# A decoder block on one core: fifteen weight pairs in place of twelve, shorter head turns, and x kept in DRAM

## The reference

```
proj = x @ w_in                               # 1024 -> 6656 channels: q | k | v | cb | cc | ch | g_conv | g_attn
y_conv = cb * conv3(cc * ch)                  # causal depthwise filter of width 3
scores = q @ k.T / 8 + alibi, window 128      # 16 query heads, 4 key/value heads of 64; 8 blocks of 128 tokens
p = exp(scores - m);  probs = p / (sum(p) + exp(sink - m))     # m = max(scores, sink)
y_attn = probs @ v
mix = (sigmoid(g_conv) * y_conv + sigmoid(g_attn) * y_attn) @ w_out
x = layer_norm(ALPHA * x + mix)
x = layer_norm(ALPHA * x + (silu(x @ w_gate) * (x @ w_up)) @ w_down)
```

## Time and profile before

| | |
|---|---|
| median of 3 runs | 1355.69 us |
| the profiled execution | 1358.13 us, span 1356.3 us |
| PE busy | 1340.0 us, 99% |
| DVE, ACT, POOL busy | 848.1, 528.0, 724.8 us |
| granted TensorE clock, mean | 0.996 |
| head turns | about 300 to 630 us of the span |
| first layer norm | about 650 to 710 us |

### The profile page before, as it was taken

One profiled execution on the slowest core, in us unless ns is written; L12 is line 12 of the kernel. 1 busy time (PEld: TensorE's weight loads), 2 busy tenths in 40 slices (PEclk: granted clock), 3 DMA queues, 4 the chain that ended last, 5 costly groups with the idle time before them and its releaser, 6 DMA issues. The chain is left out here.

```text
span 1356.3 us, 18062 instructions
## 1 busy us (share of the span) xinstructions
PE 1340.0 (99%) x6506; PEld 1176.5 (87%) x6506; DVE 848.1 (63%) x1167; ACT 528.0 (39%) x973; POOL 724.8 (53%) x487
## 2 busy tenths in 40 slices
PE   9999999999999999999899999999999999999997
PEld 8888888888888888888788888888888888888886
DVE  5665555576867778787968754545546455464547
ACT  6422322336565565755345332232322313223143
POOL 5588788721222121336682775563756637566374
PEclk9999999999999999999999999999999999999999
DMA  6111222121111111112330221211212112111113
GB/s 187 48 55 55 62 63 63 51 59 48 32 34 45 47 32 32 47 48 78 109 93 1 70 71 47 71 54 39 70 46 70 53 40 70 46 59 58 47 55 125
DMA packets 128816, 80.58 MB, mean 59 GB/s; under 512 B 8816, under 2 KB 123504, under 8 KB 128752
## 3 DMA queue, kind: packets, MB, share of 16 engines
q1 hardware_dynamic: 128752, 79.73, 19.8%
HBM read 75.53 MB, written 4.19 MB: 59 GB/s over the span
## 5 line engine op out<-in xcount | busy, mean ns | idle before, releaser
L828 POOL TENSOR_TENSOR w_lo<-raw,w_hi 128x512 fp32r<-128x512 f32 x80 | 110.3, 1379 | 204.0 <-ACT w_hi L1201 204.0
L679 POOL TENSOR_TENSOR w_lo<-raw,w_hi 128x1024 fp32r<-128x1024 f32 x28 | 68.5, 2447 | 219.9 <-ACT w_hi L887 209.9
L1664 DVE TENSOR_TENSOR res<-res,ps 128x512 f32<-128x512 f32 x128 | 87.2, 687 | 59.8 <-PE ps L1835 59.8
L1833 PE MATMUL ps<-hid_hi,wd_hi 128*128 128x512 f32 x320 | 121.5, 380 | 0.1
L1834 PE MATMUL ps<-hid_lo,wd_hi 128*128 128x512 f32 x320 | 121.3, 379 | 0.0
L1835 PE MATMUL ps<-hid_hi,wd_lo 128*128 128x512 f32 x320 | 121.3, 379 | 0.0
L2127 PE MATMUL ps<-act_hi,w_hi 128*128 128x512 f32 x320 | 121.3, 379 | 0.0
L2128 PE MATMUL ps<-act_lo,w_hi 128*128 128x512 f32 x320 | 121.3, 379 | 0.0
L2129 PE MATMUL ps<-act_hi,w_lo 128*128 128x512 f32 x320 | 121.3, 379 | 0.0
L1833 PE MATMUL ps<-act_hi,w_hi 128*128 128x512 f32 x272 | 104.5, 384 | 0.0
L1834 PE MATMUL ps<-act_lo,w_hi 128*128 128x512 f32 x272 | 103.1, 379 | 0.0
(11 more groups left out here) (262 smaller groups left out, 3590.1 us busy)
## 6 DMA issues: line engine op xcount, KB each, us to landing
raw<-in_w_in SPq DMA_DIRECT2D x28, 512.0 KB, 3.8
raw<-in_w_in SPq DMA_DIRECT2D x48, 256.0 KB, 3.0
raw<-in_w_gate SPq DMA_DIRECT2D x40, 256.0 KB, 2.8
raw<-in_w_up SPq DMA_DIRECT2D x40, 256.0 KB, 3.2
raw_d<-in_w_down SPq DMA_DIRECT2D x20, 512.0 KB, 3.4
raw<-in_w_out SPq DMA_DIRECT2D x16, 512.0 KB, 4.0
xs<-in_x SPq DMA_DIRECT2D x8, 512.0 KB, 6.9
out<-rows SPq DMA_DIRECT2D x7, 512.0 KB, 2.7
```

The costliest lines, as they stand in the source:

```text
L828: pool.tensor_tensor(wide(ring(w_lo, n)), src, fp(wide(ring(w_hi, n))), ALU.subtract).then_inc(pl_s, 1)
L1664: dve.tensor_tensor(tile, tile, bank, ALU.add).then_inc(add_s, 1)
L1833: pe.matmul(bank, w_h(t), hi, start=(t == 0), stop=False)
```

## The change

- `PLAIN = (3,)`: 15 pairs in place of 12; the odd (gc, cb) tiles of turns 0 to 2 leave the head turns, which shrink to 8 units and 8 steps for a block. Turn 3 keeps 12 units.
- New due times for short turns. On VectorE `probs_low` of a block stands at 16.3 and `gate_attention` at 24.35 steps after its start, `normalise` at 7.5.
- `sc` and `exps` become two buffers `sc_even` and `sc`, used in turn; the exponentials overwrite the scores, one element to the left. The sink column is written to both.
- x goes to DRAM (`x_away`) by two DMAs of 2 MB in the prologue and comes back by 16 DMAs of 256 KB in the output stage; `x_sum` is gone.
- Weight slots of the head turns swap parity (`head_slot`, `before_in_slot`), since an odd number of pairs ends in the other slot.
- In the first pair, GpSimd's third sum is made one place earlier. Around the first layer norm, `mean`, `variance` and `spread` are at other steps, and the normalisation is spread over more output units.

```
-PLAIN = (0, 1, 2, 3)
+PLAIN = (3,)
...
+SAME_SLOTS = HEAD_TILES.index((PLAIN[0], "gc", 1))
+
+
+def head_slot(t):
+    return (t + 1) % 2 if t < SAME_SLOTS else t % 2
...
-PE_STEPS = sorted([(block_at(b, 0), "scores", b) for b in BLOCKS] + [(block_at(b, 14, 11), "turn", b) for b in BLOCKS]
-                  + [(block_at(b, 20, 15), "values", b) for b in BLOCKS])
+PE_STEPS = sorted([(block_at(b, 0), "scores", b) for b in BLOCKS] + [(block_at(b, 14, 12.5), "turn", b) for b in BLOCKS]
+                  + [(block_at(b, 20, 20.4), "values", b) for b in BLOCKS])
...
-    [(block_at(b, 16.2, 13), "turn", b) for b in BLOCKS],
-    [(block_at(b, 22.2, 17.2), "values", b) for b in BLOCKS],
+    [(block_at(b, 16.2, 16.3), "turn", b) for b in BLOCKS],
+    [(block_at(b, 22.2, 24.35), "values", b) for b in BLOCKS],
...
-            exps = sb(st, "exps", [P, G * 2 * P + 1])
+            sc_even = sb(st, "sc_even", [P, G, 2 * P + 2])
...
-            sc = sb(st, "sc", [P, G, 2 * P + 1])
+            sc = sb(st, "sc", [P, G, 2 * P + 2])
...
+        x_away = nc.dram_tensor("x_channels", (P, DT, S), F32).ap()
...
+            sp.wait_ge(x_kept, 8)
+            sp.dma_start(x_away[:, :, half(1)], res[:, :, half(1)]).then_inc(x_stored, 16)
...
+            sp.wait_ge(x_sum0, 8)
+            sp.dma_start(x_away[:, :, half(0)], res[:, :, half(0)]).then_inc(x_stored, 16)
...
+            def x_again(h, m):
+
+                sp.wait_ge(m_lo_s, DT * h + m + 1)
+                sp.dma_start(res[:, m, half(h)], x_away[:, m, half(h)]).then_inc(x_back[DT * h + m], 16)
...
+                def third():
+                    pool.tensor_tensor(wide(block_raw(A21)), wide(block_raw(A11)), wide(block_raw(A21)),
+                                       ALU.subtract).then_inc(c_sum_s, 1)
+
                 low(FIRST_HIGH)
                 low(SECOND_SUM)
+                if c == 0:
+                    third()
                 low(SECOND_LOW)
-                pool.tensor_tensor(wide(block_raw(A21)), wide(block_raw(A11)), wide(block_raw(A21)),
-                                   ALU.subtract).then_inc(c_sum_s, 1)
+                if c:
+                    third()
...
+                    if c == 0:
+                        dve.wait_ge(x_stored, 32)
...
+                for b in range(2):
+                    dve.tensor_scalar(sc_of(b)[:, :, 2 * P + 1:],
...
-            def x_sum(h, m):
-                dve.wait_ge(m_lo_s, DT * h + m + 1)
-                dve.tensor_tensor(res[:, m, half(h)], fp(act_hi[:, m, half(h)]), fp(act_lo[:, m, half(h)]),
-                                  ALU.add).then_inc(xsum_s, 1)
...
-                dve.wait_ge(xsum_s, DT * h + m + 1)
+                dve.wait_ge(x_back[v], 16)
...
-                project_out(1, v, {DT + 1: {2: lambda: mean(0)}, DT + 3: {7: lambda: variance(0)},
-                                   DT + 4: {4: lambda: spread(0)}}.get(v, {}))
+                project_out(1, v, {DT + 1: {3: lambda: mean(0)},
+                                   DT + 3: {2: lambda: variance(0), 5: lambda: spread(0)}}.get(v, {}))
```

More of the change, by code:

```diff
@@ L140 @@
     [(-40, "weight", 0), (-33, "weight", 1)],
-    [(unit_end(last_unit(t - 2)) + 0.2, "weight", t) for t in range(2, len(HEAD_TILES))],
+    [(unit_end(last_unit(before_in_slot(t))) + 0.2, "weight", t) for t in range(2, len(HEAD_TILES))],
     [(unit_end(last_unit(len(HEAD_TILES) - 2 + v)) + 0.2, "out_weight", v) for v in range(2)],
@@ L144 @@
     [(block_at(b, 4.3), "exp", b) for b in BLOCKS],
-    [(block_at(b, 15.2, 12.1), "turn", b) for b in BLOCKS],
-    [(block_at(b, 21.2, 16.1), "values", b) for b in BLOCKS],
+    [(block_at(b, 15.2, 13.6), "turn", b) for b in BLOCKS],
+    [(block_at(b, 21.2, 21.5), "values", b) for b in BLOCKS],
     [(-30 if k == 0 else block_at(NB * k - 6, 8.1), "keys", k) for k in range(NKV)],
     [(-31 if k == 0 else block_at(NB * k - 7, 8.1), "value_rows", k) for k in range(NKV)],
-    [(LAST_TURN + 14 + 4 * m, "mix_first", m) for m in range(6)],
+    [(LAST_TURN + 24.3 + 3 * m, "mix_first", m) for m in range(6)],
     [(LAST_TURN + 63.8, "mix_first", m) for m in (6, 7)],
@@ L377, in build @@
         merge_s = sem("merge_done")
-        m_hi_s, m_lo_s, xsum_s = sem("m_hi_done"), sem("m_lo_done"), sem("x_sum_done")
+        m_hi_s, m_lo_s = sem("m_hi_done"), sem("m_lo_done")
+        x_stored = sem("x_channels_stored")
+        x_back = [sem(f"x_back{v}") for v in range(OUT_TILES)]
         out_s, res_s = sem("out_unit_done"), sem("res_tile_done")
@@ L602, in _ @@
                 load_w(v % 2, w_out, P * (v % DT))
+                for h, m in again.get(v, []):
+                    x_again(h, m)
                 if v == DT:
@@ L984, in head_weight @@
                 if t < 2:
-                    free, count = c_prod, max(n + 1 for n in range(7 * NCP) if n % 4 // 2 == t)
+                    free, count = c_prod, max(n + 1 for n in range(7 * NCP) if n % 4 // 2 == head_slot(t))
                 else:
-                    free, count = unit_s, 2 * PRO_TILES + last_unit(t - 2) + 1
-                high_part(16 * ((PRO_TILES + t) // 2 + 1), t % 2, free, count)
+                    free, count = unit_s, 2 * PRO_TILES + last_unit(before_in_slot(t)) + 1
+                high_part(16 * ((PRO_TILES + t) // 2 + 1), head_slot(t), free, count, t % 2)
             def head_unit(u):
@@ L1998, in attention_in, with slot @@
             def attention_in(first):
-                return {at - first: (lambda step=step, b=b: attend[step](b)) for at, step, b in PE_STEPS
-                        if first <= at < first + 8}
+                def slot(t):
+                    for at, step, b in PE_STEPS:
+                        if first + t <= at < first + t + 1:
+                            attend[step](b)
+                return {t: (lambda t=t: slot(t)) for t in range(8)}
             for u, (tile, h) in enumerate(UNITS):
```

104 lines of the change are left out of this document (55 added, 49 removed).

## The result

The changed kernel takes 1384.52 us in the median of 4 runs (1383.62 to 1384.75), the kernel before 1355.73 (1354.84 to 1356.12): a ratio of 1.0212, with an interval of 1.0197 to 1.0228, or 28.8 us slower. The forecast was 1383. The profiled execution took 1383.62 us with a span of 1381.8.

A forecast was written before the change was run, and what follows sets the result against it. The prediction took TensorE, busy 99% of the span, as the bound, with VectorE's loop making it wait in short turns. Terms -7.8 + 40 + 2 - 6.2 - 1.0 = +27.0 on 1355.69 gave 1382.7, say 1383; range 1366 to 1397.

The forecast's parts named there:

- The pairs, -7.8: In the conv pairs, three more pairs replace plain tiles and save TensorE matmuls: 7.8 us less.
- The turns, +40: In head turns 0 to 2, VectorE's loop outlasts TensorE's shortened work, so TensorE waits: +40 us, between 35 and 45.
- TensorE's waits: Sign in turns 0 to 2: TensorE waits in nearly each block for sums or low parts, 35 to 45 us in all.
- my sign of being wrong in size: In the turns, a clock below 1 would show the forecast wrong in size.
- Contention, +2: In the three short turns, GpSimd instructions hold up VectorE operations such as the gating: +2 us, between 0 and 8.
- The layer norm, -6.2: At the first layer norm, the 2.9 us wait for squares and the half clock after it go: -6.2 us, or 0.
- the small edits, -1.0 and 0: Second pair's weights come sooner, -1.0 us (0 to -1.8); x's stores and loads through DRAM cost 0.
- Rival A: In the short turns VectorE hides all its work and busy time decides: 15 us gained, 1341 us; 11%.
- Rival B: In the head turns the clock falls in each of 24 blocks: 26 us more, 1409 us; 9%.
- C: In the short turns the waits are partly absorbed and half of the 40 us appears: 1363 us; 7%.
- D: Whole kernel: no change, the layer norm and pairs gains meet a stall of some 15 us; 2%.

The follow-up runs named there:

- e_back: Changed kernel with before's heads' split again (four long head turns, 12 pairs, old weight slots), every other edit kept: 1350.69 us.
- e_one: Changed kernel with one exponential over all four heads of a block in place of four, leaving out the other heads' maxima and sums: 1360.14 us.
- e_lows: Changed kernel with short turns' transposed probabilities taken earlier, so VectorE subtracts their low parts before waiting for the exponentials: 1367.64 us.
- e_both: Changed kernel with the edits of e_lows and e_one together: 1344.52 us.
- e_fill: Changed kernel with six matmuls repeated in each of the 24 units of the three short turns, 31 us of extra TensorE work: 1385.08 us.
- e_pool: Changed kernel with GpSimd's low parts of the head turns' weights cut from 128x1024 to 128x128: 1378.82 us.
- e_gap: e_lows with VectorE's sums and gating of the block before also moved 3 slots earlier, behind the low parts: 1359.27 us.
- e_best: e_merge with GpSimd's low parts of the head turns' weights in short turns also waiting for the product in flight: 1346.66 us.
- e_old: Changed kernel with short turns' late steps (turned probabilities, low parts, values, sums, gating) back at before's places, ahead of the next block's reciprocal: 1418.78 us.
- e_merge: e_gap with GpSimd's two merges of a short turn waiting for VectorE's product of the block in flight: 1352.76 us.

## Why the prediction was right, and where it was off

- **The pairs, -7.8.** Right. They took 240.6 and 292.6 us, 52.0 more: 54.4 of products, less the second pair's wait of 1.8 and what else came sooner there. Against e_back, which has the other edits, it is 292.6 to 238.3, or 54.3.
- **The turns, +40.** Right in mechanism. 38.2 + 5.0 = 43.2 us were lost with the contention in it. Turns 1 and 2 took 77.4 and 76.9 us from scaling to scaling (76.9 said), turn 0 73.3 (74.5 said). The loop was 8.8 to 9.0 us in whole blocks without q (9.18 said) and 10.4 to 10.6 with it; the reciprocal waited up to 2.6. e_one and e_lows each took part of the loop away, e_both nearly all of the loss, and e_fill showed TensorE's side to be slack.
- **Two errors that offset each other.** Each short turn holds one gating that takes 1.7 to 2.0 us more than 0.43. Without this excess the turns would be some 71.4, 75.5 and 75.2 us (an estimate from these rows), 1.4 to 3.1 less than the 74.5, 76.9 and 76.9 that I had worked out without contention. So the loop was counted 6 us too long over three turns and the contention 4 us too short, and that turns 1 and 2 took just 76.9 is in part luck.
- **TensorE's waits, "35 to 45 us in all", "in nearly each block".** The row has 31.4, in 16 places, of which two lie behind turn 3's first score: 14 waits in 24 blocks. The clocks of 0.96 and 0.93 over 77 us each are another 77 x 0.11 = 8.5 us in which TensorE did nothing more: together 39.9. A slower block waits less for the same VectorE. The clock below 1 was my sign of being wrong in size; it came, and e_fill shows that it cost no time.
- **Contention, +2.** The term that was mis-sized: e_pool gave 5.7 back. I spread it as a fraction of each overlap, from a mean of 504 ns over nine gatings; in the trace of before one of the nine took 1.14 us (at 495.71) and the others 0.43. In a short turn it is one gating of 2.11 to 2.40 us in place of 0.43. The Trainium skill ("SBUF — State Buffer", "SBUF: two separate sides") has GpSimd and a VectorE instruction with two SBUF inputs exclude each other for a whole instruction; these rows and e_gap's product of 3.40 us agree. By that rule the prediction saw the term at the upper end of 0 to 8 or above; 5.7 lies nearer to that than to the 2 of the sum. The other overlaps of these turns cost nothing since they fell on operations that read PSUM, or in the hole: a part of the keys took 2.5 to 2.8 us there, unseen. Moving the GpSimd operations behind the product gave 6.5 (merges) and 6.1 us (low parts).
- **The layer norm, -6.2, and the small edits, -1.0 and 0.** The traces have -6.5 and -1.8: the wait, the half clock and the second pair's wait are gone. The margin was thinner than the 1 us that I gave it, 0.34 us here and a wait of 1.0 us in e_back. By medians the gain is smaller: e_back, with all of these edits, is 4.5 us under before, where the terms said 7.2. Both stores to DRAM landed in 8.0 us in the median and the trace shows no wait for them or for the 16 loads back.
- **The total.** By medians the short turns and the three pairs cost 33.8 us (-7.8 + 40 + 2 = 34.2 said) and the rest gained 4.5 (7.2 said). The sum of 27.0 was 1.8 us short of the measured 28.8.
- **Rival A (1341)** is what e_both and e_best come near, 1344.5 and 1346.7, once the hole is filled: right about TensorE's own need, wrong about the order as written. **Rival B**: the clock fell, but four times in 24 blocks and for 3 to 6 us each, not for whole blocks, and e_fill shows that it cost nothing. **C and D** did not occur.

What stays open: why the profiled execution of before is 2.4 us above its median, and which stage holds it. The edits at the layer norm and the copy of x in DRAM were not run apart, and neither were TensorE's and VectorE's places in e_old.

## What to carry to other kernels

An engine's busy share is not what it can deliver: add the waits that its order holds, here 2.6 us for ScalarE's exponentials in each block. Before a loop is shortened, put independent work into that hole, and see that no other engine asks for its result before it can be there: e_old had that work in the hole and lost 34 us more. Place GpSimd's long operations beside VectorE's reads of PSUM: e_merge and e_best gained 6.5 and 6.1 us by that.

## What was not expected of the hardware

After four of eight waits of 2.3 to 3.4 us amid dense matmuls the granted clock was at half for 3 to 6 us, and the same length came with and without a fall; while with 31 us more of matmuls in the same turns it stayed at 0.98 to 1.00 and the time at +0.6 us. One GpSimd operation of 2.4 us stretched a VectorE operation with two SBUF operands from 0.43 to 2.26 us or from 1.23 to 3.40, and left a scaling or a subtraction out of PSUM at 1.23 and 1.41 us.
